# B vectors and tables of the state-space tiles made by POOL during the feed-forward, and doubled by ACT tile by tile

## The chip, the cores and the metric

The kernel runs on one core of one Trainium2 chip. Its engines are TensorE (PE), VectorE (DVE), ScalarE (ACT), GpSimd (POOL) and SyncE (SP), which here only issues transfers. The metric is the device time of one execution in microseconds, the median of several runs. The profile is of one execution more, taken by the hardware profiler.

## What is computed

One sequence of 256 tokens with 1,024 features goes through two layers of a first block (feed-forward, mixer, feed-forward) and two layers of a second block (attention, a dense feed-forward, a mixture of experts). The change touches only the mixer of the first block, and there only its S5 branch, a diagonal complex state-space model with 64 groups of 16 channels and 64 states:

```python
for i in range(DEPTH):                       # DEPTH = 2
    f = swiglu(rmsnorm(h, ffn1_pre_g[i]), ...)
    h = h + 0.5 * rmsnorm(f, ffn1_post_g[i])
    m = mixer(rmsnorm(h, mix_pre_g[i]), ...)  # ssd_branch and s5_branch
    h = h + rmsnorm(m, mix_post_g[i])
    ...
def s5_branch(u, ...):
    lam_bar = jnp.exp(lam * step)
    b_bar = ((lam_bar - 1.0) / lam)[..., None] * lax.complex(b_re, b_im)
    bu = jnp.einsum("blgc,gnc->blgn", ug, b_bar)
    _, states = lax.associative_scan(combine, (a_elems, bu), axis=1)
    y = jnp.real(jnp.einsum("blgn,gcn->blgc", states, c))
    ...
```

## The kernel before

All products are made from a high and a low part of each operand. For a chunk of weights (2,048 elements in each of 128 partitions) SP loads `raw`, ACT copies it to `w_hi` (line 1177), DVE subtracts to get `w_lo` (line 1634), and PE takes the chunk in three passes (lines 618 to 620, 671). Three slots go round, so the converts of a tick make the chunk that PE uses three ticks later. Each engine runs a program of its own, written out by hand in program order; only semaphores tie them together.

The first feed-forward has 11 steps (0 to 10) of three chunks. In a step, ACT applies SiLU twice, DVE makes `k_hi`, `stage` and `k_lo` of two hidden tiles (lines 1699 and 1687) and then converts. Behind some steps each engine does parts of the S5 set-up, by the tables handed to `ffn(...)`: DVE makes the powers and projections behind steps 6 and 7, the B vectors of tile 0 and a rotation table behind step 8, two more tables behind step 9. Then comes the post-norm and the next pre-norm: DVE lines 1675, 1677 (products with the gain, source in PSUM), 1680 (H updated), 1657 (H scaled into G), 1666 (low parts), with ACT between them; PE fills the time with `warm` matmuls (line 614), turns the stream (line 680) and starts the mixer.

The mixer goes in ticks, one chunk each: 4 for `u`, 1 for `dt`, 8 gates, 12 for the convolution, 8 for `z`. The S5 branch is spread over the ticks in 8 tiles of four pairs of groups. For tile t, PE turns the masked C (line 736) and the B vectors (line 743, `in_psum`) in tick 2t + 1, makes the local products (line 753, `local_psum`) and the chunk inputs (line 762) in tick 2t + 2, and the output (lines 774, 779) in tick 2t + 4. DVE makes the C vectors in tick 2t + 1 (`s5_cvecs`, lines 1859 to 1863) and scans in tick 2t + 3 (`s5_scan`, lines 1880 to 1894); tables for rotating the state (`s5_table`, lines 1872 to 1874) come in the ticks that `S5_TABLE_AT` names. In tick 7 DVE also makes the softplus of `dt` (`softplus_and_sums`), and taps of the convolution (line 1907) from tick 14 on. ACT masks the inputs (line 1291) and the diagonal (line 1300), fills the damping (line 1310), applies GELU (line 1315), evicts each chunk and converts. In tick 6 it waits twice for DVE (`dt_step`, lines 1370 and 1372).

POOL makes the B vectors of tiles 1 to 7 inside the mixer: two products of 512 elements once PE has turned the tile before (lines 2381, 2382), and once the local products of the tile before are through, a sum that writes each value twice, 1,024 elements (line 2385). Later it masks decays of the other branch (line 2372).

## Time and profile before

| what | us |
|---|---|
| median of three runs | 3162.09 |
| lowest and highest of them | 3159.95, 3169.51 |
| the profiled execution | 3172.73 |
| its span, first to last instruction | 3170.9 |
| PE busy | 3008.0 |
| DVE busy | 2228.4 |
| ACT busy | 1702.4 |
| POOL busy | 157.9 |

The granted clock of PE was 0.973 on average. In the page's 40 slices POOL works in four around 238 to 555 us and in three around 1110 to 1427 us: the two mixers of the first block, the only places with S5 tiles. Layer 1 repeats layer 0 about 897 us later. A row of a timeline gives start, duration, engine, line, operation, tiles and in brackets the idle time before it with what ended it.

### The profile page before, as it was taken

Reading aid. Unit: us, or ns where it says so; the run is one execution under the profiler, and the core shown is the slowest. Engines: PE = TensorE matmul, PEld = TensorE weight load, DVE = VectorE, ACT = ScalarE, POOL = GpSimd, SP = SyncE. Lnnn points to the kernel's source line nnn. Section 1 sums busy time; section 2 is a strip of 40 time slices with the busy share of each in tenths; the row PEclk is TensorE's granted clock in tenths of the full one; section 3 lists DMA queues with packets and bytes.
Section 4 is the critical chain, followed back from the end, with each engine's and each line's share of the span. In section 5 each row is a group of like instructions: output and inputs, shape, how many; then the busy total and the mean of one; then the engine's idle time right before and its main releaser. Section 6 shows DMA issues by size and latency. Waiting matters only on the chain.

```text
span 3170.9 us, 52654 instructions
## 1 busy us (share of the span) xinstructions
PE 3008.0 (95%) x20975; PEld 2688.3 (85%) x20975; DVE 2228.4 (70%) x2557; ACT 1702.4 (54%) x1966; POOL 157.9 (5%) x110
## 2 busy tenths in 40 slices
PE   8998999999989989998999999999799999999997
PEld 7998998989989978988989897999587877777776
DVE  5779975655557789957555555555568888888887
ACT  4445666334444456663344444444456776667665
POOL 0002213000000022030000000000000000000000
PEclk9998999999999999999999999999889999999999
DMA  7553352446545533533555453555079999999995
GB/s 227 173 156 92 111 155 81 157 139 208 174 154 194 167 112 94 143 111 107 168 170 194 163 186 120 186 171 181 6 260 363 330 342 350 327 326 344 351 326 200
DMA packets 488737, 619.92 MB, mean 196 GB/s; under 512 B 34689, under 2 KB 439059, under 8 KB 488595
## 3 DMA queue, kind: packets, MB, share of 16 engines
q1 hardware_dynamic: 488595, 617.91, 59.4%
q8 instruction: 104, 1.70, 0.2%
q14 instruction: 38, 0.31, 0.0%
HBM read 616.81 MB, written 1.05 MB: 195 GB/s over the span
## 4 chain that ended last, share of the span: by engine, by line
PE 76%; DVE 15%; ACT 4%; issue 3%; SPq 1%; DMA 0%; DVEq 0%; ACTq 0%
PE PS L1077 13%; PE PS L618 12%; PE PS L620 12%; PE PS L619 12%; PE PS L671 11%; DVE w_lo L1634 3%; PE PS L1102 3%; PE PS L1104 3%; PE PS L1103 3%; ACT w_hi L1177 1%; PE PS L1054 1%; ACT w_hi L1566 1%; PE PS L1112 1%; PE PS L800 1%; DVE act_out L1887 1%
## 5 line engine op out<-in xcount | busy, mean ns | idle before, releaser
L618 PE MATMUL PS<-x_hi,w_hi 128*128 128x256 f32 x3360 | 970.7, 289 | 17.7 <-DVE x_lo L1666 9.2
L619 PE MATMUL PS<-x_hi,w_lo 128*128 128x256 f32 x3360 | 961.4, 286 | 0.0
L620 PE MATMUL PS<-x_lo,w_hi 128*128 128x256 f32 x3360 | 960.8, 286 | 0.0
L1634 DVE TENSOR_TENSOR w_lo<-raw,w_hi 128x2048 fp32r<-128x2048 f32 x313 | 720.0, 2316 | 314.0 <-ACT w_hi L1177 313.3
L1177 ACT ACTIVATE w_hi<-raw 128x2048 fp32r<-128x2048 f32 x313 | 598.7, 1913 | 402.3 <-PE PS L671 249.0
L618 PEld LDWEIGHTS PS<-x_hi,w_hi 128*128 128x128 f32 x3360 | 656.3, 195 | 28.6 <-issue 13.3
L619 PEld LDWEIGHTS PS<-x_hi,w_lo 128*128 128x128 f32 x3360 | 656.5, 195 | 1.9
L620 PEld LDWEIGHTS PS<-x_lo,w_hi 128*128 128x128 f32 x3360 | 655.7, 195 | 0.0
L1077 PE MATMUL PS<-w_hi,x_hi 128*128 128x512 f32 x704 | 284.8, 405 | 3.1 <-DVE stage L2283 2.3
L1077 PE MATMUL PS<-w_lo,x_hi 128*128 128x512 f32 x704 | 276.4, 393 | 0.0
L1077 PE MATMUL PS<-w_hi,x_lo 128*128 128x512 f32 x704 | 274.9, 390 | 0.0
L1699 DVE TENSOR_TENSOR k_hi<-act_out,PS 128x256 fp32r<-128x256 f32 x110 | 46.2, 420 | 280.6 <-PE PS L620 279.0
L2277 DVE TENSOR_TENSOR w_lo<-raw,w_hi 128x2048 fp32r<-128x2048 f32 x96 | 219.9, 2290 | 32.6 <-ACT w_hi L1566 31.6
L2277 DVE TENSOR_TENSOR w_lo<-XC,w_hi 128x2048 fp32r<-128x2048 f32 x88 | 201.7, 2293 | 34.0 <-ACT w_hi L1566 31.8
L1566 ACT ACTIVATE w_hi<-raw 128x2048 fp32r<-128x2048 f32 x96 | 183.7, 1914 | 15.5 <-PE PS L1104 14.1
L671 PE MATMUL PS<-w_hi,k_hi 128*128 128x512 f32 x568 | 180.2, 399 | 6.4 <-DVE k_lo L1982 5.0
L671 PE MATMUL PS<-w_lo,k_hi 128*128 128x512 f32 x568 | 178.0, 395 | 0.0
L671 PE MATMUL PS<-w_hi,k_lo 128*128 128x512 f32 x568 | 177.3, 394 | 0.0
L1231 ACT ACTIVATE act_out<-PS 128x256 f32<-128x256 f32 x55 | 21.1, 384 | 279.2 <-PE PS L620 279.2
L1566 ACT ACTIVATE w_hi<-XC 128x2048 fp32r<-128x2048 f32 x88 | 168.2, 1912 | 1.2 <-DMA XC<-in_w_gu_moe_dram 1.2
L1077 PEld LDWEIGHTS PS<-w_hi,x_hi 128*128 128x128 f32 x704 | 132.6, 188 | 31.2 <-issue 3.7
L1077 PEld LDWEIGHTS PS<-w_lo,x_hi 128*128 128x128 f32 x704 | 132.4, 188 | 29.6
(410 smaller groups left out, 4715.0 us busy)
## 6 DMA issues: line engine op xcount, KB each, us to landing
XC<-in_w_gu_moe_dram SPq DMA_DIRECT2D x176, 512.0 KB, 8.9
raw<-in_w_gu_moe_dram SPq DMA_DIRECT2D x132, 512.0 KB, 7.9
raw<-in_w_in_dram SPq DMA_DIRECT2D x64, 1024.0 KB, 5.7
raw<-in_ffn_w_gate_dram SPq DMA_DIRECT2D x44, 1024.0 KB, 5.4
raw<-in_ffn_w_up_dram SPq DMA_DIRECT2D x44, 1024.0 KB, 6.4
raw<-in_ffn_w_down_dram SPq DMA_DIRECT2D x44, 1024.0 KB, 4.9
raw<-in_w_down_moe_dram SPq DMA_DIRECT2D x32, 1024.0 KB, 9.9
G<-in_w_down_moe_dram SPq DMA_DIRECT2D x32, 1024.0 KB, 9.5
```

The costliest lines, as they stand in the source:

```text
L618: mm(dst, w_hi[:, slot, w0:w0 + P], hi, start=start, stop=False, skip_group_check=True)
L619: mm(dst, w_lo[:, slot, w0:w0 + P], hi, start=False, stop=False, skip_group_check=True)
L620: return mm(dst, w_hi[:, slot, w0:w0 + P], lo, start=False, stop=True, skip_group_check=True)
L671: last = mm(PS[:, bank + 2 * t + b, :], left, right[:, slot, kt * D + 512 * b:kt * D + 512 * (b + 1)], start=False, stop=True, skip_group_ ...
L1077: last = mm(PS[:, 4, :], left, right, start=(k0 + k == 0 and right is whi and left is hi), stop=True, skip_group_check=True)
L1102: mm(PS[:, b, :], hi, whi, start=False, stop=True, skip_group_check=True)
L1103: mm(PS[:, b, :], lo, whi, start=False, stop=True, skip_group_check=True)
L1104: last = mm(PS[:, b, :], hi, wlo, start=False, stop=True, skip_group_check=True)
L1177: fn(w_hi[:, slot, :], raw[:, slot, :], ACT.Copy).then_inc(s["hi_ready"], n.one("hi_ready"))
L1566: fn(w_hi[:, MOE_SLOT[kind], :], MOE_RAW[kind][j % 3], ACT.Copy).then_inc(s["hi_ready"], n.one("hi_ready"))
L1634: tt(w_lo[:, slot, :], raw[:, slot, :], w_hi[:, slot, :].bitcast(F32), SUB)\
L2277: tt(w_lo[:, slot, :], MOE_RAW[kind][j % 3], w_hi[:, slot, :].bitcast(F32), SUB)\
```

## The change

POOL's program begins in the feed-forward. Once DVE has made the powers and projections (a new semaphore, `powers_ready`, behind step 7) and ACT the sines and cosines, POOL makes the five tables 0 to 4 and then the B vectors of tiles 0 to 4 in short form: 512 elements a tile, with the sum written once. DVE's `s5_first_bvecs` and the tables behind steps 8 and 9 and in ticks 0 and 1 are gone. ACT gets `s5_expand(t)`: it waits for `b_made` and copies the 512 elements of a tile to the 1,024 of `bvecs`, tile 0 behind step 9 of the feed-forward, tile t in tick 2t + 1. DVE waits for all five at the start of the mixer. Tiles 5 and 6 POOL makes after the fourth scan, tile 7 after the sixth doubling. The scratch of the norms' squares moves from `G` to `work`, since `G` now holds short B vectors. The core of the diff:

```diff
-S5_TABLE_AT = {0: 3, 1: 4, 4: 7, 6: 5, 8: 6}
+S5_TABLE_AT = {4: 7, 6: 5, 8: 6}
+S5_AHEAD = 5
...
-        weighted, scaled, unused = by_token(U5[:, :, :]), by_token(G[:, 0:8, :]), by_token(G[:, 8:16, :])
+        weighted, scaled = by_token(U5[:, :, :]), by_token(G[:, 0:8, :])
+        unused = wk(2368, 2, D)
...
+            def s5_expand(t):
+                act.wait_ge(s["b_made"], n.due("b_made"))
+                both = lambda x: x.rearrange("p (m c) -> p m c", c=16)[:, :, None, :].to_broadcast([P, 32, 2, 16])
+                fn(bvecs.rearrange("p w (q g c) -> p (w q) g c", q=4, g=2), both(b_homes[t]), ACT.Copy)\
+                    .then_inc(s["b_ready"], n.one("b_ready"))
...
-                else:
-                    act.wait_ge(s["b_ready"], n.due("b_ready"))
...
-                if i == 2:
-                    act.wait_ge(s["b_ready"], n.due("b_ready", S5_TILES - 1))
...
-                    for first, part in ((2, s5_inputs), (3, s5_diagonal), (0, s5_masked), (5, gelu)):
+                    for first, part in ((2, s5_inputs), (3, s5_diagonal), (1, s5_expand), (0, s5_masked), (5, gelu)):
...
-                ffn({3: (s5_exps,), 4: (s5_angles,), 6: (s5_tables,)})
+                ffn({3: (s5_exps,), 4: (s5_angles,), 6: (s5_tables,), 9: (lambda: s5_expand(0),)})
...
-                then(v.memset(damping[:, :, 0:1], 0.0))
...
+                v.memset(damping[:, :, 0:1], 0.0).then_inc(s["powers_ready"], n.one("powers_ready"))
+                dve.wait_ge(s["powers_ready"], n.last("powers_ready"))
...
+                dve.wait_ge(s["b_made"], n.due("b_made", S5_AHEAD))
...
-                     7: (s5_projections,), 8: (s5_first_bvecs, *tables_at(0)), 9: (*tables_at(1, 2), lambda: v.memset(local, 0.0))})
+                     7: (s5_projections,), 9: (lambda: v.memset(local, 0.0),)})
...
-                tt(a_, part(0), coef(powers_a), MULT)
-                then(tt(b_, part(1), coef(powers_b), MULT))
-                pair = lambda x: x.rearrange("p w q c -> p (w q) c")[:, :, None, :].to_broadcast([P, 32, 2, 16])
-                pool.wait_ge(s["local_psum"], n.due("local_psum"))
-                tt(bvecs.rearrange("p w (q g c) -> p (w q) g c", q=4, g=2), pair(a_), pair(b_), ADD)\
-                    .then_inc(s["b_ready"], n.one("b_ready"))
-                pool.wait_ge(s["b_ready"], n.last("b_ready"))
+                tt(dst, part(0), coef(powers_a), MULT)
+                then(tt(tmp, part(1), coef(powers_b), MULT))
+                tt(dst, dst, tmp, ADD).then_inc(s["b_made"], n.one("b_made"))
+                pool.wait_ge(s["b_made"], n.last("b_made"))
...
+                pool.wait_ge(s["powers_ready"], n.due("powers_ready"))
+                pool.wait_ge(s["table_ready"], n.due("table_ready"))
+                for t in range(5):
+                    s5_table(t)
+                for t in range(S5_AHEAD):
                     s5_bvecs(t)
...
+                pool.wait_ge(s["h5_ready"], n.due("h5_ready", 4))
+                s5_bvecs(5)
+                s5_bvecs(6)
+                pool.wait_ge(s["b_ready"], n.due("b_ready", 6))
+                s5_bvecs(7)
```

`s5_table` is the function that DVE had, word for word, with a scratch buffer of `work` as its temporary.

POOL's program in layer 0 before, from its first product for tile 1 in tick 2 of the mixer on:

```order
L2381 TENSOR_TENSOR G<-XC,work 128x512 [waits in_psum]
L2382 TENSOR_TENSOR G<-XC,work 128x512
L2385 TENSOR_TENSOR work<-G 128x1024 [waits local_psum,pool_step]
L2381 TENSOR_TENSOR G<-XC,work 128x512 [waits in_psum,b_ready]
L2382 TENSOR_TENSOR G<-XC,work 128x512
L2385 TENSOR_TENSOR work<-G 128x1024 [waits local_psum,pool_step]
```

And now, from the last of its five tables (lines 2373 to 2375), behind which come the B vectors of tiles 0 and 1:

```order
L2373 TENSOR_TENSOR XC<-work 128x512 [waits pool_step]
L2374 TENSOR_TENSOR work<-work 128x512
L2375 TENSOR_TENSOR XC<-XC,work 128x512 [waits pool_step]
L2383 TENSOR_TENSOR work<-XC,work 128x512 [waits pool_step]
L2384 TENSOR_TENSOR work<-XC,work 128x512
L2385 TENSOR_TENSOR work<-work 128x512 [waits pool_step]
L2383 TENSOR_TENSOR G<-XC,work 128x512 [waits b_made]
L2384 TENSOR_TENSOR work<-XC,work 128x512
L2385 TENSOR_TENSOR G<-G,work 128x512 [waits pool_step]
```

The waits for PE inside the mixer are gone, the operations are all of 512 elements, and nothing but POOL itself holds one back once the first has started.

DVE's program behind the converts of step 8 of the feed-forward, before: the B vectors of tile 0 and the first of three tables (the other two stood behind step 9).

```order
L1846 TENSOR_TENSOR work<-XC,work 128x512
L1847 TENSOR_TENSOR work<-XC,work 128x512
L1849 TENSOR_TENSOR work<-work 128x1024 [waits dve_step]
L1872 TENSOR_TENSOR XC<-work 128x512 [waits table_ready,b_ready]
L1873 TENSOR_TENSOR work<-work 128x512
L1874 TENSOR_TENSOR XC<-XC,work 128x512 [waits dve_step]
```

And now, behind step 9 up to the post-norm:

```order
L2066 MEMSET XC 128x512
L1705 TENSOR_TENSOR k_hi<-act_out,PS 128x256 [waits up_a,silu_done]
L1705 TENSOR_TENSOR stage<-act_out,PS 128x256
L1693 TENSOR_TENSOR k_lo<-stage,k_hi 128x256 [waits dve_step]
L1705 TENSOR_TENSOR k_hi<-act_out,PS 128x256 [waits chunk_used,silu_done]
L1705 TENSOR_TENSOR stage<-act_out,PS 128x256
L1693 TENSOR_TENSOR k_lo<-stage,k_hi 128x256 [waits dve_step]
L1640 TENSOR_TENSOR w_lo<-raw,w_hi 128x2048 [waits hi_ready] x2
L1681 TENSOR_TENSOR U<-PS,conv_out 128x1024 [waits chunk_used,gain_in]
```

The B vectors and the tables have left; the order of the rest is the same.

ACT's program in ticks 2 and 3 of the mixer, before (line 1300 masks the diagonal, line 1385 is the eviction, line 1177 the convert):

```order
L1385 ACTIVATE U<-PS 128x512 [waits chunk_used]
L1177 ACTIVATE w_hi<-raw 128x2048 [waits chunk_used,raw_c]
L1310 ACTIVATE rstd<-s5c 128x4x63 [waits b_ready]
L1300 ACTIVATE XC<-PS,con 32x4x16 [waits local_psum]
L1300 ACTIVATE XC<-PS,con 32x4x16 x7
L1385 ACTIVATE U<-PS 128x512 [waits chunk_used]
L1177 ACTIVATE w_hi<-raw 128x2048 [waits chunk_used,raw_a]
```

And now (lines 1304, 1391 and 1181 are the same operations, line 1312 is the doubling):

```order
L1391 ACTIVATE U<-PS 128x512 [waits chunk_used]
L1181 ACTIVATE w_hi<-raw 128x2048 [waits chunk_used,raw_c]
L1318 ACTIVATE rstd<-s5c 128x4x63
L1304 ACTIVATE XC<-PS,con 32x4x16 [waits local_psum]
L1304 ACTIVATE XC<-PS,con 32x4x16 x7
L1312 ACTIVATE work<-G 128x1024 [waits b_made]
L1391 ACTIVATE U<-PS 128x512 [waits chunk_used]
L1181 ACTIVATE w_hi<-raw 128x2048 [waits chunk_used,raw_a]
```

The doubling is new between the diagonal and the eviction, and line 1318 has lost its wait for `b_ready`.

## Rows read from the trace of the kernel before

**Rows 1.** Who waited for whom, PE, 230 to 400 us: total, times, longest.

```profile
PE PS L753 <- DVE work L1863: 8.2, 5, 2.4
PE PS L762 <- ACT XC L1291: 5.6, 1, 5.6
```

**Rows 2.** Windows, scan 0 to C vectors 7, both layers: length, busy PE, PEld, DVE, ACT, POOL, PE clock.

```profile
248.28:390.93 142.65, 124.82 (x1678) 120.33 (x1676) 134.66 (x160) 85.86 (x140) 35.88 (x18) 0.90 0.33 99
1145.27:1291.00 145.73, 124.08 (x1678) 119.50 (x1677) 138.92 (x160) 85.71 (x140) 37.85 (x18) 0.92 0.34 96
```

**Rows 3.** Timelines of DVE and POOL: start, duration, engine, line, operation, shapes, idle before.

```profile
229.11 0.69 DVE L1872 TENSOR_TENSOR XC<-work 128x512 f32<-128x512 f32 x1
...
236.84 1.49 DVE L1859 TENSOR_TENSOR work<-PS,work 128x1280 f32<-128x1280 f32 x1
236.98 1.11 POOL L2381 TENSOR_TENSOR G<-XC,work 128x512 f32<-128x512 f32 x1 [236.53 <-PE PS L743]
...
261.40 3.68 POOL L2385 TENSOR_TENSOR work<-G 128x1024 f32<-128x1024 f32 x1 [6.33 <-PE PS L753]
262.76 2.86 DVE L1872 TENSOR_TENSOR XC<-work 128x512 f32<-128x512 f32 x1
```

**Rows 4.** Timeline of DVE: softplus up to the scan; scan, taps, C vectors, next convert.

```profile
294.65 0.27 DVE L1917 TENSOR_SCALAR rows<-rows 32x256 f32<-32x256 f32 x1
...
300.65 0.67 DVE L1880 TENSOR_TENSOR work<-PS,XC 128x512 f32<-128x512 f32 x1
...
377.71 0.68 DVE L1880 TENSOR_TENSOR work<-PS,XC 128x512 f32<-128x512 f32 x1
...
383.51 2.71 DVE L1907 SCALAR_TENSOR_TENSOR conv_out<-conv_in,prm,conv_out 128x256 f32<-128x256 f32 x6
386.14 1.48 DVE L1859 TENSOR_TENSOR work<-PS,work 128x1280 f32<-128x1280 f32 x1
...
390.97 2.29 DVE L1634 TENSOR_TENSOR w_lo<-raw,w_hi 128x2048 fp32r<-128x2048 f32 x1
```

**Rows 5.** Timeline of DVE, its only idle times in the stretches of rows 2.

```profile
292.44 2.29 DVE L1634 TENSOR_TENSOR w_lo<-raw,w_hi 128x2048 fp32r<-128x2048 f32 x1 [4.06 <-ACT w_hi L1177]
...
354.77 2.29 DVE L1634 TENSOR_TENSOR w_lo<-raw,w_hi 128x2048 fp32r<-128x2048 f32 x1 [1.18 <-ACT w_hi L1177]
...
1189.48 2.29 DVE L1634 TENSOR_TENSOR w_lo<-raw,w_hi 128x2048 fp32r<-128x2048 f32 x1 [4.05 <-ACT w_hi L1177]
```

**Rows 6.** Groups by line with shapes apart, POOL: busy, mean ns, idle before.

```profile
L2385 POOL TENSOR_TENSOR work<-G 128x1024 f32<-128x1024 f32 x8 | 27.7, 3468 | 52.8 <-PE PS L753 52.8
```

**Rows 7.** Timelines of DVE and ACT, end of the feed-forward and the norms.

```profile
168.50 0.06 DVE L1839 MEMSET rstd<- 128x4 f32 x1
...
204.25 0.38 ACT L1231 ACTIVATE act_out<-PS 128x256 f32<-128x256 f32 x1 [5.38 <-PE PS L620]
...
208.33 4.49 DVE L1634 TENSOR_TENSOR w_lo<-raw,w_hi 128x2048 fp32r<-128x2048 f32 x2
...
215.66 2.48 DVE L1680 SCALAR_TENSOR_TENSOR H<-U,sums,H 128x1024 f32<-128x1024 f32 x2
216.98 1.06 ACT L1193 ACTIVATE G<-H 128x1024 f32<-128x1024 f32 x1 [1.55 <-DVE H L1680]
219.88 1.42 DVE L1657 TENSOR_SCALAR G<-H,sums 128x1024 f32<-128x1024 f32 x2
```

**Rows 8.** Timeline of PE: transposes and first chunks, before the mixer and before layer 1.

```profile
220.69 1.97 PE L680 MATMUL PS<-con,G 128*128 128x128 f32 x16 [1.23 <-DVE G L1657]
223.84 0.39 PE L618 MATMUL PS<-x_hi,w_hi 128*128 128x256 f32 x1 [1.18 <-DVE x_lo L1666]
...
235.64 0.38 PE L736 MATMUL PS<-con,stage 128*128 128x128 f32 x2
...
911.88 3.68 PE L680 MATMUL PS<-con,G 128*128 128x128 f32 x16 [7.72 <-DVE G L1657]
...
920.83 0.41 PE L618 MATMUL PS<-x_hi,w_hi 128*128 128x256 f32 x1
```

More of the change, by code:

```diff
@@ L1372, in mixer @@
                         fn(dt_rows[:, 3, :], dt_rows[:, 2, :], ACT.Ln).then_inc(s["dt_act"], n.one("dt_act"))
-                    for first, part in ((2, s5_inputs), (3, s5_diagonal), (0, s5_masked), (5, gelu)):
+                    for first, part in ((2, s5_inputs), (3, s5_diagonal), (1, s5_expand), (0, s5_masked), (5, gelu)):
                         t = s5_at(k, first)
-                        if t is not None:
+                        if t is not None and not (part == s5_expand and t == 0):
                             part(t)
@@ L1838, in s5_projections @@
                 v.memset(h5[:, :, :, 0:1], 0.0)
-                then(v.memset(damping[:, :, 0:1], 0.0))
-            def s5_first_bvecs():
-                q = slice(0, 4)
-                a_, b_ = (x[:, 0:512].rearrange("p (w q c) -> p w q c", w=8, q=4) for x in s5_tmp)
-                part = lambda r: b_raw[:, r, None, q, :].to_broadcast([P, 8, 4, 16])
-                coef = lambda x: x[:, q, :].rearrange("p q w -> p w q")[:, :, :, None].to_broadcast([P, 8, 4, 16])
-                tt(a_, part(0), coef(powers_a), MULT)
-                then(tt(b_, part(1), coef(powers_b), MULT))
-                pair = lambda x: x.rearrange("p w q c -> p (w q) c")[:, :, None, :].to_broadcast([P, 32, 2, 16])
-                tt(bvecs.rearrange("p w (q g c) -> p (w q) g c", q=4, g=2), pair(a_), pair(b_), ADD)                    .then_inc(s["b_ready"], n.one("b_ready"))
-                dve.wait_ge(s["b_ready"], n.last("b_ready"))
+                v.memset(damping[:, :, 0:1], 0.0).then_inc(s["powers_ready"], n.one("powers_ready"))
+                dve.wait_ge(s["powers_ready"], n.last("powers_ready"))
             def s5_cvecs(t):
@@ L2018, in mixer @@
                     convert((MIX + k) % RING)
-                n.given["b_ready"] += S5_TILES - 1
+                n.due("b_made", S5_TILES - S5_AHEAD)
                 ssd_inputs(7)
@@ L2069, in _ @@
                 pos[0] = -1
-                tables_at = lambda *tiles: tuple((lambda t=t: s5_table(t)) for t in tiles)
                 ffn({2: (s5_rows_a,), 3: (s5_rows_b,), 4: (s5_rows_c,), 5: (s5_columns, s5_turns), 6: (s5_powers,),
-                     7: (s5_projections,), 8: (s5_first_bvecs, *tables_at(0)), 9: (*tables_at(1, 2), lambda: v.memset(local, 0.0))})
+                     7: (s5_projections,), 9: (lambda: v.memset(local, 0.0),)})
                 post_norm()
@@ L2372, in ssd_masks, with s5_table @@
                     tt(d, d, gmask[:, (i // 2) % 2, :], MULT).then_inc(s["masked"], n.one("masked"))
+            def s5_table(t):
+                q = slice(4 * t, 4 * t + 4)
+                tmp = b_scratch[0].rearrange("p (q h l) -> p q h l", q=4, l=8)
+                dst = tables[t].rearrange("p q r (h l) -> p q (r h) l", l=8)
+                tt(dst, high_a[:, q, :, None].to_broadcast([P, 4, 16, 8]), low_cos[:, q, None, :].to_broadcast([P, 4, 16, 8]), MULT)
+                then(tt(tmp, high_b[:, q, :, None].to_broadcast([P, 4, 16, 8]), low_sin[:, q, None, :].to_broadcast([P, 4, 16, 8]), MULT))
+                then(tt(dst, dst, tmp, ADD))
@@ L2374, in s5_bvecs @@
             def s5_bvecs(t):
-                pool.wait_ge(s["in_psum"], n.due("in_psum"))
                 q = slice(4 * t, 4 * t + 4)
-                a_, b_ = (b_parts[t > 4][:, 512 * i:512 * (i + 1)].rearrange("p (w q c) -> p w q c", w=8, q=4) for i in range(2))
+                dst, tmp = (x.rearrange("p (w q c) -> p w q c", w=8, q=4) for x in (b_homes[t], b_scratch[t]))
                 part = lambda r: b_raw[:, r, None, q, :].to_broadcast([P, 8, 4, 16])
                 coef = lambda x: x[:, q, :].rearrange("p q w -> p w q")[:, :, :, None].to_broadcast([P, 8, 4, 16])
-                tt(a_, part(0), coef(powers_a), MULT)
@@ L2382, in s5_bvecs @@
-                then(tt(b_, part(1), coef(powers_b), MULT))
-                pair = lambda x: x.rearrange("p w q c -> p (w q) c")[:, :, None, :].to_broadcast([P, 32, 2, 16])
-                pool.wait_ge(s["local_psum"], n.due("local_psum"))
-                tt(bvecs.rearrange("p w (q g c) -> p (w q) g c", q=4, g=2), pair(a_), pair(b_), ADD)\
-                    .then_inc(s["b_ready"], n.one("b_ready"))
-                pool.wait_ge(s["b_ready"], n.last("b_ready"))
-            for l in range(DEPTH):
-                n.given["b_ready"] += 1
-                for t in range(1, S5_TILES):
-                    s5_bvecs(t)
-                n.due("in_psum")
-                n.due("local_psum")
+                tt(dst, part(0), coef(powers_a), MULT)
```

10 lines of the change are left out of this document (6 added, 4 removed).

## The prediction

> **What bounds the kernel now.** I read the list of waits of TensorE (PE) over layer 0's mixer first, then the windows that give each engine's busy time over the state-space part, then the timelines of DVE and POOL side by side. PE is busy nearly everywhere, so only its idle stretches matter. In the mixer it waits 8.2 us in five pieces for DVE's projected C vectors (line 1863) and 5.6 us in one for ACT's masked inputs, which hang on DVE too [rows 1]. From the first scan to the last C vectors, 142.65 us in layer 0 and 145.73 us in layer 1, DVE is busy 134.66 and 138.92 us, PE only 124.8 and 124.1 [rows 2]. DVE is the bound there.
>
> But DVE is not busy with work of its own all that time. A table operation takes 0.69 us alone and 2.86 us when it starts under POOL's 3.68 us operation; POOL's own span has grown as well, since it began under DVE's convert [rows 3]. A DVE operation with two SBUF sources and a POOL operation stand in turn, a whole instruction at a time. An operation that reads PSUM runs beside POOL at its usual 1.49 us [rows 3].
>
> **DVE's own work in the stretch.** A scan is 383.51 - 377.71 = 5.80 us, the taps 386.14 - 383.51 = 2.63, a tile's C vectors 390.97 - 386.14 = 4.83, the softplus 300.65 - 294.65 = 6.0 [rows 4]; a convert is 2.2 (two in 4.49 [rows 7]), a table three times 0.69, 2.07 [rows 3]. By the ticks there lie in it 12 converts (26.4), 7 scans (40.6), 7 sets of C vectors (33.8), the 3 tables of ticks 4, 6, 8 (6.2), two taps (5.3), the softplus (6.0) and two small operations (0.6, estimated at half a table operation each): 118.9 us. DVE waits for ACT's high parts 4.06 + 1.18 us in layer 0 and 4.05 in layer 1 [rows 5]. The rest, 142.65 - 118.9 - 5.2 = 18.5 us and 145.73 - 118.9 - 4.1 = 22.7 us, is what POOL costs DVE: 0.52 and 0.60 of POOL's busy 35.88 and 37.85 us [rows 2].
>
> **Part 1, the mixer.** POOL's B vectors of tiles 1 to 4 leave the mixer, and the doubling operation over 1,024 elements (mean 3.47 us [rows 6]) leaves POOL altogether. Tiles 5, 6 and 7 stay, in short form: 9 operations of 1.11 us [rows 3], 10.0 us of POOL. At the shares above (0.55) they cost DVE 5.5 us; the bounds are 2 us (all under operations that read PSUM) and 10 us (each in full). DVE's stretch becomes 118.9 + 5.5 + 4.1 = 128.5 us. The wait of 4.1 stays: ACT sits in tick 6 behind DVE's `dt_step` and then has its chain before the next high part, whatever POOL does. So layer 0 gains 142.65 - 128.5 = 14.2 us and layer 1 gains 17.2: 31.4 us. This counts on PE, which needs 124 us there with its slow pieces in, less than 128.5.
>
> ACT takes on the doubling: one copy of 1,024 elements a tile, 1.06 us by the row of the same length [rows 7]. It stands in the odd ticks behind the masking of the diagonal, which waits for PE in any case; behind it are queued the eviction and ACT's convert. PE wants the vectors after the whole chunk of that tick, some 5.9 us later (two chunks in 235.64 - 223.84 = 11.8 [rows 8]). I price it at nothing; if that cover went it would be 1.06 us x 7 a layer. The two tables leaving DVE's ticks 0 and 1 bring nothing: in both ticks DVE then waits for ACT or PE.
>
> **Part 2, the end of the feed-forward.** POOL starts when DVE has the powers, at 168.5 us [rows 7], and has 30 operations: 15 for five tables, 15 for five tiles. Up to the last convert's end, 212.8 us, there are 44.3 us. DVE has 8 converts and 6 small two-SBUF operations in that time (8 x 2.2 + 6 x 0.35 = 19.7 us, the small ones estimated at half a table operation), so POOL has 24.6 us for itself: at 1.11 us, and one semaphore step of about 0.1 (estimated) in three, 21 to 22 operations. Eight or nine are left when the post-norm begins. Within steps 8 and 9 the delays, one POOL operation before each convert, fall into DVE's waits; I charge 0.2 us a layer. In step 10 there is no such room: the two converts run straight into the post-norm, which PE waits for. One POOL operation goes before each: 2.2 us. The two updates of H (2.48 us [rows 7]) and the two scalings to G (1.42) come next on the path: half of four operations of 1.11, 2.2 us; the small low part 0.2. The sum is 4.6 us a layer. The bounds are 3.4 (the updates and scalings meet nothing more than one operation) and 9 (each of the seven meets one and POOL's operations are longer).
>
> The POOL work taken off DVE in steps 8 and 9 gives nothing, for DVE waits for PE there. ACT's first doubling stands between step 9's last convert and step 10's first SiLU and waits for the 18th POOL operation. At 1.11 us and under the converts that operation ends at about 203 us; the doubling then ends about 204, and ACT's second SiLU of that step starts at 204.25 in any case [rows 7]. Nothing, with little to spare (rival B). The wait of DVE at the mixer's start, for five tiles, is met: POOL is done at about 224 us, DVE gets there at 231 or later.
>
> **Part 3, the clock.** PE covers the post-norm with 32 dummy matmuls and idles 1.23 us before the turning of the stream at 220.69 [rows 8]. With 4.6 us more this idle is 5.8 us. In front of layer 1, after an idle of 7.72 us, the same 16 transposes took 3.68 us in place of 1.97, at the lower of the two clock levels (1.2 instead of 2.4 GHz), and the matmuls behind them started late as well: from the transposes' start to the 22nd matmul 920.83 - 911.88 = 8.95 us [rows 8]. At full clock it is 223.84 - 220.69 = 3.15 and 21 x 0.123 = 2.6, together 5.7. I charge 3.2 us a layer; the bounds are 0 (the clock holds over 5.8 us) and 4.
>
> **Sum.** -31.4 + 2 x (4.6 + 0.2 + 3.2) = -15.4 us. The profiled execution took 3172.7 us with a span of 3170.9, 10 us above the median of the three runs, and nothing in the sum depends on that; against the median 3162.1 - 15.4 = 3147 us.
>
> **What the Trainium skill would say.** POOL does the 512 elements in 1.11 us and DVE in 0.69, a ratio of 1.6 [rows 3]. The page "GPSIMD Engine Reference", section "3.1 Elementwise — side-by-side cycle accounting", gives 1.96 for a two-input operation over 2,048 elements. By that ratio each would be 1.35 us, an estimate of that page's, and the time would be that of rival A. The row is nearer, and the sum goes by it.
>
> **Rivals.**
> A, the lock only changes its place. Each moved operation that still meets DVE costs what it cost before, now at the norm where nothing covers it. If POOL's operations are 1.2 to 1.3 us long, 12 are left at 212.8 and each of the seven DVE operations meets one; a convert of steps 8 and 9 is late by 0.5 us or so. A layer pays 9 + 1 + 4 = 14, the sum is -31.4 + 28 = -3.4: 3159 us. For it speaks that DVE has no slack between 208.33 and 215; against it that POOL's short operation is 1.11. The Trainium skill ("Perfetto Trace Analysis", "Optimizing Scalar/DVE Operations") warns that work moved between these two engines may bring nothing, since they share a port; that is this rival.
> B, slower. ACT is held at its first doubling. It has room until about 204.5 us, by that SiLU; from there each us is PE's, because step 10's last products need the SiLU. With L us of lateness the change costs 2 x (L + 8) and breaks even at L = 7.7, which is POOL operations of about 1.5 us with these broadcast operands, which the trace shows only in another arrangement. At 1.7 us the 18th ends near 217, L = 12, and the norm loses 9: -31.4 + 2 x (12 + 9 + 1 + 4) = +20.6: 3183 us.
> C, the clock holds over the longer idle, or POOL's nine operations in the mixer hide under PSUM reads: -6.4 and -7: 3134 to 3141 us.
> D, something else bounds the mixer once DVE is lighter: PE after its slow pieces, or ACT with the doublings. Then the stretch is 132 us, the gain 24.5, the time 3154.
>
> **Chances.** Forecast (3141 to 3152) 0.46, C 0.16, A 0.16, D 0.12, B 0.10. The range reaches from C's lower end to above A: 3132 to 3164. A measurement of this kernel tells about 0.3%, 9.5 us, from no change. Faster by more: the forecast and C, 0.62. Within: A and D, 0.27 (with the weakest part of B). Slower: 0.11.
>
> **What would show it.** In the profile after: the stretch from scan 0 to C vectors 7 at about 128 us, with POOL's operations gone from ticks 3 to 8 and DVE's 2.86 us table at 0.69; the wait of PE for L1291's successor still there. POOL's 30 operations from 168.5 to about 224 us at 1.1 to 1.5 us each. The norm's DVE operations about 4.6 us later, PE's idle before the transposes 5 to 6 us and the granted clock at half behind it. Wrong it would be if ACT stood more than 6 us before its first doubling, if PE idled in step 10, or if the stretch stayed over 135 us.

## The result and the profile after

The changed kernel takes 3130.2 us (median of four runs, 3121.7 to 3136.2) where the kernel before takes 3162.6 (3160.0 to 3169.5). The ratio is 0.9891, with a 95% interval of 0.9875 to 0.9907. It is faster by 32.4 us, where 15.4 were forecast; the range ended at 3132, 1.8 us too high. The profiled execution took 3136.2 us with a span of 3134.4, so the two profiled executions lie 36.5 us apart.

The windows from scan 0 to the last C vectors answer to [rows 2], with the same columns:

```profile
249.10:378.81 129.71, 120.01 (x1626) 116.29 (x1625) 120.73 (x160) 89.89 (x145) 16.14 (x9) 0.95 0.35 109
1137.64:1265.00 127.36, 118.48 (x1686) 115.19 (x1684) 120.55 (x160) 91.40 (x146) 16.11 (x9) 0.96 0.38 111
```

142.65 us have become 129.71, and 145.73 have become 127.36: 12.9 and 18.4 us less, 31.3 together, where 31.4 were forecast. DVE's busy time fell by 13.9 and 18.4 us with the same 160 operations, so it was indeed waiting time inside busy operations that went. PE's clock rose from 0.90 and 0.92 to 0.95 and 0.96.

The timelines of POOL and DVE at the end of the feed-forward and in the norm, layer 0, answer to [rows 7] (start, duration, engine, line, operation, shapes, idle before):

```profile
165.83 1.07 POOL L2373 TENSOR_TENSOR XC<-work 128x512 f32<-128x512 f32 x1 [165.38 <-DVE rstd L1845]
...
173.29 3.00 POOL L2373 TENSOR_TENSOR XC<-work 128x512 f32<-128x512 f32 x1
176.26 3.11 POOL L2374 TENSOR_TENSOR work<-work 128x512 f32<-128x512 f32 x1
179.45 3.23 POOL L2375 TENSOR_TENSOR XC<-XC,work 128x512 f32<-128x512 f32 x1
...
185.00 1.31 POOL L2375 TENSOR_TENSOR XC<-XC,work 128x512 f32<-128x512 f32 x1
...
217.82 2.12 POOL L2385 TENSOR_TENSOR G<-G,work 128x512 f32<-128x512 f32 x1
```

```profile
171.98 9.54 DVE L1640 TENSOR_TENSOR w_lo<-raw,w_hi 128x2048 fp32r<-128x2048 f32 x3
...
205.71 6.52 DVE L1640 TENSOR_TENSOR w_lo<-raw,w_hi 128x2048 fp32r<-128x2048 f32 x2
212.15 1.21 DVE L1681 TENSOR_TENSOR U<-PS,conv_out 128x1024 f32<-128x1024 f32 x1
...
215.07 3.75 DVE L1686 SCALAR_TENSOR_TENSOR H<-U,sums,H 128x1024 f32<-128x1024 f32 x2
220.57 1.42 DVE L1663 TENSOR_SCALAR G<-H,sums 128x1024 f32<-128x1024 f32 x2
```

The turns can be read off. Alone, a product of a table lasts 1.07 us on POOL and its sum 1.31; under a convert each shows 3.0 to 3.2; three converts with POOL beside them take 9.54 us. In step 10 two converts take 6.52 instead of 4.49 us and the two updates of H 3.75 instead of 2.48. The product that reads PSUM (line 1681) is as short as ever, and so are the scalings into G, for POOL ended at 217.82 + 2.12 = 219.94 us.

PE and ACT around it answer to [rows 8] and [rows 7]: the transposes and first chunks of both layers, and ACT's first doubling.

```profile
221.38 3.68 PE L684 MATMUL PS<-con,G 128*128 128x128 f32 x16 [4.62 <-DVE G L1663]
225.61 0.43 PE L622 MATMUL PS<-x_hi,w_hi 128*128 128x256 f32 x1 [0.56 <-DVE x_lo L1672]
...
1112.60 0.58 PE L622 MATMUL PS<-x_hi,w_hi 128*128 128x256 f32 x1 [0.56 <-DVE x_lo L1672]
```

```profile
199.49 1.06 ACT L1312 ACTIVATE work<-work 128x1024 f32<-128x1024 f32 x1 [4.67 <-POOL work L2385]
200.46 0.36 ACT L1233 ACTIVATE act_out<-PS 128x256 f32<-128x256 f32 x1
```

PE idles 4.62 us before the transposes, which then run at the lower clock (3.68 us in place of 1.97). In layer 0 the clock is back for the first matmuls behind them (0.12 us apart); in layer 1 the first of them takes 0.58 us. PE's list of waits from 230 to 390 us answers to [rows 1]:

```profile
PE PS L747 <- DVE work L1875: 3.5, 1, 3.5
PE PS L766 <- ACT XC L1295: 3.5, 1, 3.5
PE PS L757 <- DVE work L1859: 2.7, 3, 1.8
```

The wait for the C vectors (now line 1859) is down from 8.2 us to 2.7.

The next table cuts every profiled execution at the same operations of DVE. "Norm" runs from the powers (POOL's start) over step 10 and the norms to scan 0, "stretch" from scan 0 to the start of the last C vectors (4.8 us shorter than the windows above). Both are given for layer 0 and layer 1, and "rest" is all else.

| kernel | norm | stretch | rest | span |
|---|---|---|---|---|
| before | 79.8, 79.8 | 137.9, 141.0 | 2732.5 | 3170.9 |
| before_again | 79.8, 79.8 | 140.3, 141.0 | 2723.9 | 3164.8 |
| changed | 83.4, 84.9 | 124.9, 122.6 | 2718.6 | 3134.4 |
| after_again | 83.1, 84.7 | 122.9, 122.6 | 2717.5 | 3130.9 |
| bvecs_only | 79.7, 79.7 | 122.6, 122.6 | 2713.5 | 3118.1 |
| short_in_mixer | 78.8, 78.8 | 129.3, 129.4 | 2713.8 | 3130.2 |
| no_pool_in_mixer | 85.0, 84.9 | 121.4, 120.6 | 2708.7 | 3120.5 |
| nine_more_behind | 83.6, 85.1 | 123.0, 122.6 | 2720.7 | 3135.0 |
| nine_more_ahead | 93.9, 91.6 | 122.9, 122.6 | 2708.8 | 3139.8 |
| warm48 | 91.3, 91.3 | 123.0, 122.6 | 2716.2 | 3144.3 |
| warm24 | 82.3, 82.3 | 124.9, 122.6 | 2710.3 | 3122.5 |
| step_early | 79.7, 79.6 | 118.8, 118.8 | 2714.2 | 3111.1 |
| before_no_pool | 78.8, 78.8 | 120.7, 120.7 | 2711.9 | 3110.9 |
| softplus_behind | 79.7, 79.7 | 119.5, 119.2 | 2721.8 | 3119.9 |

The rest spreads over 13 us among the kernels other than before, which do the same there. From the last C vectors in layer 0 to the powers of layer 1 the traces show 678.7 us with 13.7 us lost to the lower clock, and 670.5 us with 5.1 lost, for one and the same kernel (changed, after_again). I take such losses as the length times one minus the granted clock, summed over short windows. The length without them is 665 us both times. So the norm and the stretch are what a single trace can tell; the rest it can't.

### The profile page after: what moved, and what is told of

Same layout as the page of the kernel before. It is cut to its first block, busy times and chain, and to the rows that moved or that the text cites. A ratio compares the mean times of both kernels' runs of the same rounds, so it can differ in the third digit from the quotient of the medians.

```text
span 3134.4 us, 52666 instructions
## 1 busy us (share of the span) xinstructions
PE 2988.7 (95%) x20975; PEld 2672.7 (85%) x20975; DVE 2189.0 (70%) x2521; ACT 1716.8 (55%) x1982; POOL 211.7 (7%) x146
## 4 chain that ended last, share of the span: by engine, by line
PE 78%; DVE 14%; ACT 4%; issue 3%; DVEq 0%; DMA 0%; SPq 0%; ACTq 0%
PE PS L1081 13%; PE PS L622 12%; PE PS L623 12%; PE PS L624 12%; PE PS L675 11%; DVE w_lo L1640 3%; PE PS L1106 3%; PE PS L1108 3%; PE PS L1107 3%; ACT w_hi L1181 1%; PE PS L1058 1%; ACT w_hi L1572 1%; PE PS L804 1%; PE PS L1116 1%; DVE act_out L1881 1%
## 5 line engine op out<-in xcount | busy, mean ns | idle before, releaser
L1640 DVE TENSOR_TENSOR w_lo<-raw,w_hi 128x2048 fp32r<-128x2048 f32 x313 | 730.0, 2349 | 303.1 <-ACT w_hi L1181 302.4
L2271 DVE TENSOR_TENSOR w_lo<-raw,w_hi 128x2048 fp32r<-128x2048 f32 x96 | 219.8, 2289 | 32.6 <-ACT w_hi L1572 32.4
```

What stands on the lines that cost most here:

```text
L1640: tt(w_lo[:, slot, :], raw[:, slot, :], w_hi[:, slot, :].bitcast(F32), SUB)\
L2271: tt(w_lo[:, slot, :], MOE_RAW[kind][j % 3], w_hi[:, slot, :].bitcast(F32), SUB)\
```

## Experiments

### The two kernels once more

> The changed kernel once more, word for word. Expected: 0.989 of before again, 3125 to 3135 us. The stretch from scan 0 to the last C vectors again 129.7 and 127.4 us within 1 us, the way from POOL's start to the post-norm again 2.2 us longer than before in both layers. If the 2.8 us that the changed kernel was ahead before POOL had started (165.69 in place of 168.50) and the 5.6 us of layer 1's last third are chance, they differ here; if they belong to the change they repeat.

Measured: 3132.5 us (five runs), ratio 0.9896 (0.9877 to 0.9914).

> The kernel before once more, word for word, for its trace alone: which stretches repeat and which do not. Expected: scan 0 to the start of the last C vectors 137.9 and 141.0 us within 1, post-norm to the low parts 10.2, first low part to scan 0 25.4. If the long way from layer 0's last C vectors to layer 1's powers (679.35 us) and from layer 1's last C vectors to the end (1884.6) come out otherwise, the 10 us between the profiled execution and the median are in them.

Measured: a span of 3164.8 us. In both kernels the norm repeats within 0.3 us and layer 1's stretch within 0.1; layer 0's differs by 2.0 us between the traces of the changed kernel and by 2.5 between those of before. The 2.8 us by which the changed kernel was ahead at the powers are chance: all traces together reach that point between 164.3 and 168.5 us, before_again at 167.1. The 5.6 us of layer 1 did not repeat either: from the last C vectors of layer 1 to the end the second trace of the changed kernel took 1880.7 us, the first 1874.2.

### Only the B vectors on POOL

```diff
-S5_TABLE_AT = {4: 7, 6: 5, 8: 6}
+S5_TABLE_AT = {0: 3, 1: 4, 4: 7, 6: 5, 8: 6}
...
-                     7: (s5_projections,), 9: (lambda: v.memset(local, 0.0),)})
+                     7: (s5_projections,), 8: tables_at(0), 9: (*tables_at(1, 2), lambda: v.memset(local, 0.0),)})
...
-                pool.wait_ge(s["table_ready"], n.due("table_ready"))
-                for t in range(5):
-                    s5_table(t)
```

> POOL makes only the B vectors of tiles 0 to 4 in the feed-forward (15 operations in place of 30), DVE makes the tables where it made them before. Theory (the cost of the change is POOL's work that reaches into step 10 and the norm): POOL is done by about 192 us, the two converts of step 10 take 4.5 us again, PE idles 1.2 us before the transposes at full clock, the stretch from scan 0 to the last C vectors stays at 128 to 130 us. Gain over the changed kernel 3.5 + 1.1 us in layer 0 and 3.4 + 2.6 in layer 1: 10.6 us, to about 3120 us. Rival (DVE has no room for tables 3 and 4 in ticks 0 and 1 any more): the first scan comes 2 to 4 us later a layer than the norm's end allows, and the gain is 3 to 6 us.

Measured: 3123.8 us (five runs), ratio 0.9868 (0.9846 to 0.9890); the changed kernel, measured beside it, 3132.5. Windows of layer 0 from the powers to the post-norm, and from there to the low parts (columns as in [rows 2]), first the changed kernel's:

```profile
165.69:212.15 46.46, 46.46 (x315) 43.26 (x314) 33.74 (x31) 20.47 (x18) 45.06 (x26) 1.00 0.49 160
212.15:224.68 12.53, 7.91 (x38) 6.99 (x36) 7.84 (x9) 4.87 (x11) 7.56 (x5) 0.77 0.31 98
```

```profile
165.69:210.76 45.07, 44.68 (x305) 41.45 (x304) 39.19 (x39) 19.49 (x17) 26.79 (x15) 1.00 0.49 160
210.76:220.94 10.18, 8.70 (x48) 7.31 (x46) 6.58 (x9) 5.86 (x13) 0.00 (x0) 1.00 0.45 139
```

With 15 operations POOL is out of the way before step 10, and the norm takes its old 10.18 us at full clock. From the powers to the post-norm it is 45.07 us, 0.8 more than in the kernel before: here DVE makes tables in steps 8 and 9 too, and POOL's turns there do show. The stretch is what it was in the changed kernel, 122.6 us. The norm column of the table falls by 3.7 and 5.2 us, 8.9 together (10.6 were expected), and the medians by 8.7. The rival, that DVE has no room for two tables in ticks 0 and 1, is out: from the low parts to scan 0 it takes 24.42 us, as without them. The tables on POOL bring nothing and cost all that the norm pays.

### Only the short form and the doubling

```diff
+        b_homes = [wk(3904, 512)] + [flat(G[:, 12:14, :])] * 4 + [
...
-                pool.wait_ge(s["table_ready"], n.due("table_ready"))
-                for t in range(5):
-                    s5_table(t)
-                for t in range(S5_AHEAD):
+                s5_bvecs(0)
+                for t in range(1, S5_TILES):
+                    pool.wait_ge(s["in_psum"], n.due("in_psum"))
+                    if t == 7:
+                        pool.wait_ge(s["b_ready"], n.due("b_ready", 6))
                     s5_bvecs(t)
...
```

The tables are on DVE here, as in bvecs_only.

> Half of the change: ACT doubles as in the changed kernel, but POOL makes the B vectors of tiles 1 to 7 in the mixer, in the ticks where it made them before, in short form; tables on DVE as before. Theory (POOL's busy time in the stretch times 0.55 is what DVE loses): 21 operations of 1.11 us, 23.3 us, cost 12.8; the stretch is 118.9 + 12.8 + 4.1 = 135.8 us, between before (142.65, 145.73) and the changed kernel (129.7, 127.4); the norm is as before. In time about 2 x 8.4 = 17 us under before, 3145. Rival (it was the 1,024-element operation that hurt, since it started under a convert and blocked the C vectors): the stretch is 131 us or less, the time 3130.

Measured: 3132.6 us (six runs), ratio 0.9898 (0.9875 to 0.9922). Windows of the stretch (to the start of the last C vectors), in this kernel, in the kernel before and in before_no_pool (below):

```profile
243.16:372.49 129.33, 117.61 (x1593) 114.42 (x1592) 119.77 (x155) 87.92 (x141) 24.74 (x18) 0.92 0.37 112
```

```profile
248.28:386.14 137.86, 121.71 (x1600) 117.50 (x1599) 129.97 (x155) 81.62 (x134) 35.88 (x18) 0.90 0.34 102
```

```profile
244.30:364.95 120.65, 113.74 (x1588) 110.90 (x1587) 111.51 (x155) 80.41 (x134) 0.00 (x0) 0.96 0.39 119
```

The stretch to the end of the C vectors is 134.1 us (129.3 + 4.8), where the theory said 135.8 and the rival 131 or less: nearer the theory. POOL still makes 18 operations there. But the time as a whole, which I had put at 3145 and the rival at 3130, is that of the changed kernel. Norm and stretch account for 23 of the 35 us gained, on the mean of the two traces of before; the remainder is of the kind left open below. Without POOL at step 10 the norm is short (78.8 us), so what the stretch loses against the changed kernel (6.1 us a layer) the norm gives back (5.2). In the change as it was made, then, B vectors and tables together, moving POOL's work out of the mixer has brought nothing measurable. What it gains net is what this kernel gains too: the third operation, 1,024 elements on POOL behind a wait for the local products, became 512 without that wait and a copy on ACT. Which of the two it is, the length or the wait, this run does not separate.

That does not hold for the B vectors alone. The kernel bvecs_only differs from this one in where POOL makes them. Its stretch is 6.7 us a layer shorter (122.6 for 129.3), its norm 0.9 longer, and its median is 8.8 us lower. So the move is worth something; in the changed kernel the tables, moved along, eat it up at the norm.

### What POOL costs in the mixer, before and after

The kernel before with POOL's `s5_bvecs` emptied:

```diff
-                tt(a_, part(0), coef(powers_a), MULT)
-                then(tt(b_, part(1), coef(powers_b), MULT))
...
-                tt(bvecs.rearrange("p w (q g c) -> p (w q) g c", q=4, g=2), pair(a_), pair(b_), ADD)\
-                    .then_inc(s["b_ready"], n.one("b_ready"))
-                pool.wait_ge(s["b_ready"], n.last("b_ready"))
+                pool.sem_inc(s["b_ready"], 1)
+                n.given["b_ready"] += 1
```

> The kernel before with POOL's operations in the mixer left out: the B vectors of tiles 1 to 7 are not computed, those of tile 0 stay in the buffer; POOL only waits and signals. Theory (POOL's 35.9 us a layer cost DVE 18.5 to 22.7 us of the stretch, and ACT's doubling costs nothing): from scan 0 to the start of the last C vectors 137.9 to 141.0 us fall to 120.6 to 121.4, as in the kernel without POOL's nine operations, where ACT doubles. If it comes out at 117 or less, the doubling on ACT does cost 4 us a layer or more; if at 125 or more, something else than POOL was in before's stretch.

Measured: 3111.0 us (four runs), ratio 0.9838 (0.9812 to 0.9864), stretch 120.65 and 120.68 us.

The changed kernel without the nine operations that POOL has left in the mixer:

```diff
-                s5_bvecs(5)
-                s5_bvecs(6)
+                pool.sem_inc(s["b_made"], 2)
+                n.given["b_made"] += 2
                 pool.wait_ge(s["b_ready"], n.due("b_ready", 6))
-                s5_bvecs(7)
+                pool.sem_inc(s["b_made"], 1)
+                n.given["b_made"] += 1
```

> The changed kernel with POOL's nine operations for tiles 5 to 7 left out: the B vectors of these tiles are not computed, ACT doubles what lies in their buffers. Theory: the stretch falls by the 5.5 us that they were priced at, to 123 to 124 us a layer, and the time by 11 us. Rival (PE, busy 124 us, bounds it then, or the nine lay under operations that read PSUM): it falls by 2 us or less a layer.

Measured: 3126.4 us (four runs), ratio 0.9876 (0.9855 to 0.9897), stretch 121.4 and 120.6.

Both end at the same stretch, one with ACT's doubling and one without: the doubling is hidden. POOL's work cost the kernel before 17.2 and 20.3 us of the stretch. DVE's busy time without it is 111.5 us, so before it held 18.5 and 22.8 us of waiting for POOL. The prediction had worked out 18.5 and 22.7, and that agreement is luck: it took DVE's own work 2.6 us too high and its idle time too low (5.2 and 4.1 us, where the stretch of before has 7.9 and 6.7). The nine operations that are left cost 2.2 us a layer (123.25, the mean of four stretches, less 121.0), not 5.5: about what the rival said. They add 4.4 us to DVE's busy time (115.9 for 111.5), but the stretch grows by half of that only; the other half comes off DVE's idle time.

### POOL at work through the norm, and ahead of the first doubling

```diff
                 for t in range(S5_AHEAD):
+                    if t == S5_AHEAD - 1:
+                        for again in range(3):
+                            s5_table(4)
                     s5_bvecs(t)
```

> The changed kernel with nine POOL operations more (table 4 three times again) ahead of the B vectors of tile 4, so that POOL works on through the norm. Theory of the forecast (the scaling of H into G meets POOL as well): the two scalings take 3.6 us in place of 1.42, post-norm to low parts 14.7 in place of 12.5 us, and with the clock 2 to 4 us a layer in all. Rival (an operation with one SBUF tensor and a scalar a row does not take turns with POOL): the scalings stay at 1.42 us, and the norm costs what it did.

Measured: 3131.8 us (four runs), ratio 0.9897 (0.9870 to 0.9923). The scalings into G:

```profile
219.06 2.55 DVE L1663 TENSOR_SCALAR G<-H,sums 128x1024 f32<-128x1024 f32 x2
```

They take 2.55 us in place of 1.42 (I had expected 3.6): an operation with a single SBUF tensor takes turns with POOL too, once for the two. The rival is out. This agrees with the Trainium skill: the page "SBUF — State Buffer", section "🔬 SBUF: two separate sides", has DVE and GpSimd share one pair of ports under an exclusive lock, taken by DVE operations with two SBUF inputs or in a two-port mode, for a whole instruction; the products from PSUM at 1.21 us fit it as well. But the norm lengthens by 0.3 us only (12.80 for 12.53 us from post-norm to low parts, where I had expected 14.7), since PE begins the transposes after the first scaling and at the low clock needs longer than the second takes. So even with POOL at work there, the scalings would have cost the norm 0.3 us, and not the 1.1 that is their half of my 2.2.

```diff
-                for t in range(5):
+                for t in (0, 1, 2, 3, 4, 4, 4, 4):
                     s5_table(t)
```

> The changed kernel with nine POOL operations more (table 4 three times again) ahead of all B vectors. Theory (rival B of the prediction, ACT held at its first doubling): tile 0 is ready 10 to 12 us later, at 210 us instead of 199.5, the first SiLU of step 10 stands behind it, PE idles 6 to 9 us in step 10, and the time grows by 15 to 24 us with the norm's part. If it grows by less than 8, ACT's place behind step 9 has more room than the prediction gave it.

Measured: 3144.6 us (eight runs), ratio 0.9947 (0.9931 to 0.9963). ACT's doubling and the matmul of step 10 behind it:

```profile
208.84 1.06 ACT L1312 ACTIVATE work<-work 128x1024 f32<-128x1024 f32 x1 [15.24 <-POOL work L2385]
```

```profile
211.46 1.22 PE L675 MATMUL PS<-w_hi,k_hi 128*128 128x512 f32 x2 [8.32 <-DVE k_lo L1693]
```

Rival B of the prediction is a real mechanism. The doubling starts 10.6 us later after the powers (208.84 - 164.47 = 44.4 for 199.49 - 165.69 = 33.8) and PE idles 8.32 us: the room was 2.2 us, where the prediction had about half a microsecond. Up to the post-norm the kernel takes 9.0 and 8.1 us longer than the changed one, in the median 13 us (against 3131.8 with the nine behind, measured beside it), a little under the 15 to 24 expected. Still it is faster than the kernel before, since the gain of the stretch stands against it.

### The clock

```diff
                 ffn(rows=True)
-                warm(4, 16)
+                warm(4, 48)
```

> The changed kernel with 48 dummy matmuls in place of 16 at the place ahead of the transposes of the norm. Theory (the idle of 4.6 us is what lets the clock fall): PE idles 1.2 us there, the transposes take 1.97 us, low parts 1.1 us earlier, the way from there to scan 0 is 24.4 us in both layers (25.97 and 24.42 in the changed kernel). Gain 2 to 5 us a kernel: 3128 us. Rival (the clock falls anyhow): nothing.

Measured: 3145.6 us (six runs), ratio 0.9946 (0.9928 to 0.9964). I had mis-sized it: 32 dummy matmuls more are not 3.4 us but 11.3, and the norm grew to 91.3 us. It tells only the price of one, 0.35 us, and that with PE busy the way to scan 0 is 24.40 us in both layers.

> The changed kernel with 24 dummy matmuls in place of 16 ahead of the transposes (the profile shows each as two: 48 for 32). With 48 in place of 16 the post-norm to the first low part grew from 12.5 to 20.4 us, so one costs 0.35 us on PE (11.3 us for 32, with the 4.6 us of idle used up first 3.4): eight are 2.8 us. Theory: PE idles 1.8 us before the transposes, they take 1.97 us, the first low part comes 11.4 to 11.5 us after the post-norm's start, and from there to scan 0 it is 24.4 us in both layers (24.4 to 26.0 in the changed kernel). Gain 2 to 5 us over the changed kernel. Rival (the clock falls anyhow): nothing.

Measured: 3127.0 us (five runs), ratio 0.9874 (0.9852 to 0.9896).

```profile
219.99 1.97 PE L684 MATMUL PS<-con,G 128*128 128x128 f32 x16 [1.17 <-DVE G L1663]
```

The idle is 1.17 us, the transposes take 1.97, and the norm column is 82.3 in both layers, 1.1 and 2.6 us less than in the changed kernel: the clock term. It is the idle that lets the clock fall, and a few more dummies take it back. How long it stays down is not the same each time: in layer 0 of two executions of the same kernel it was back by the end of the transposes, in layer 1 of both some 17 matmuls later, and in no_pool_in_mixer, which does the same there, late in both layers (norm 85.0 and 84.9).

### What bounds the mixer next

This kernel is bvecs_only with one operation of DVE in another place:

```diff
-                    if k == 6:
-                        dve.wait_ge(s["dt_act"], n.due("dt_act"))
-                        ts(dt_rows[:, 2, :], dt_rows[:, 1, :], 1.0, None, ADD).then_inc(s["dt_step"], n.one("dt_step"))
                     t = s5_at(k, 3)
                     if t is not None:
                         s5_scan(t)
+                    if k == 5:
+                        dve.wait_ge(s["dt_act"], n.due("dt_act"))
+                        ts(dt_rows[:, 2, :], dt_rows[:, 1, :], 1.0, None, ADD).then_inc(s["dt_step"], n.one("dt_step"))
```

> bvecs_only (POOL makes the B vectors of tiles 0 to 4 in the feed-forward, DVE all tables) with one DVE operation moved: the second dt_step, that ACT waits 5.9 us for in tick 6, stands in tick 5 between scan 1 and the C vectors of tile 2, and no longer at the head of tick 6. Theory (ACT's wait in tick 6 is what DVE's 4.1 us for the high part and PE's 3.5 and 2.7 us hang on): ACT waits under 1 us there, DVE's wait falls under 1 us, PE's two waits under 1.5 us together, the stretch from scan 0 to the start of the last C vectors falls from 122.6 to 117 to 119 us a layer. Time 3123.8 - 2 x 4.5, about 3115. Rival (PE is the bound by now): the waits move to another line and the time stays at 3120 or above.

Measured: 3112.0 us (five runs, 3111.0 to 3115.3), ratio 0.9828 (0.9808 to 0.9847), the fastest complete kernel of this study. ACT's second step in the changed kernel and here:

```profile
279.68 0.42 ACT L1378 ACTIVATE rows<-rows 32x256 f32<-32x256 f32 x1 [5.93 <-DVE rows L1990]
```

```profile
268.77 0.42 ACT L1378 ACTIVATE rows<-rows 32x256 f32<-32x256 f32 x1
```

The 5.93 us are gone, and with them PE's wait for the masked inputs; DVE's for the high part is down to 1.1 us. The stretch fell from 122.6 to 118.8 us a layer, as the theory said, and the rival is out. But PE kept a long wait between 245 and 380 us, beside 1.4 us in three short ones; the expectation was under 1.5 us in all:

```profile
PE PS L747 <- DVE work L1877: 5.1, 1, 5.1
```

It hangs on scan 2, which stands behind the softplus in tick 7. The last kernel turns these two round.

```diff
-                    if k == 7:
-                        softplus_and_sums()
                     t = s5_at(k, 3)
                     if t is not None:
                         s5_scan(t)
+                    if k == 7:
+                        softplus_and_sums()
```

> step_early with the softplus of tick 7 behind scan 2 in place of ahead of it. In step_early PE waits 5.1 us in tick 7 for that scan to have read its inputs. Theory (DVE's own work is the bound: 118.9 us and about 2 for POOL's nine, of the 123.6 from scan 0 to the end of the last C vectors): PE's wait falls under 1 us, but the stretch from scan 0 to the start of the last C vectors falls by 0 to 2.6 us only, 116.2 to 118.8, and the time by 5 us at most. Rival (PE's wait was the last one that counted): the stretch falls by 4 us or more, to 114 or less, the time to 3104 or less.

Measured: 3120.9 us (five runs), ratio 0.9847 (0.9823 to 0.9871). The stretch is 119.5 and 119.2 us, not shorter, and the list of waits from 245 to 380 us reads

```profile
PE PS L757 <- DVE work L1859: 6.5, 3, 5.5
```

PE's wait did not fall under 1 us as expected, it moved to the C vectors. DVE is busy 116 of 119.4 us, so it is the bound and PE's waits only show where. That fits the theory, though its range for the stretch (116.2 to 118.8) is missed by 0.4 and 0.7 us, and the rival is out. At a stretch 0.5 us longer than step_early's, the 9 us between the medians are not from here: two of the five runs took 3109.1 and 3109.4 us, less than any of step_early, and three 3120.9 to 3121.7. The trace is one of the three; it has 7.6 us more in the rest, 5 of them time lost to the lower clock. The order of the two operations is not shown to cost anything.

## Why the prediction was wrong

The direction and the mechanism were right, but the gain forecast, 15.4 us, was half of what was measured. The step that failed is the price of the norm: parts 2 and 3 charged 16.0 us for it, and it cost 8.7. The lower-clock time behind the stretch was put at nothing, and part of the miss stays open. By the steps of the prediction, on the two profiled executions:

**Part 1, the mixer: 31.4 us forecast, 31.3 measured.** The sum holds, but three of its terms were off and cancelled. To the start of the last C vectors, DVE's own work is 111.5 us where I had 118.9 - 4.8 = 114.1. POOL's nine operations cost 2.2, not 5.5: I carried the share of 0.55 over from a POOL program of long operations, and the bound "all under PSUM reads", 2 us, was the better value. And DVE's idle time without POOL is 9.1 us (120.65 - 111.5), not 4.1: three waits for ACT's high parts make 7.1 of it, and the rest is short gaps between operations. That the sum came out within 0.1 us is luck.

**Part 2, step 10 and the norm: 4.8 us a layer forecast, 3.5 measured.** The converts were right (2.2 forecast, 2.0 measured). The updates of H took 1.27 us more, and the scalings nothing, since POOL was done at 219.94 and not at 224. That is the term mis-sized: eight or nine operations were to be left at the post-norm, and 26 of 30 had been issued when it began. I had counted the small operations of DVE as blocking POOL, which they hardly do, and the converts at 2.2 us each: eight converts at 1.95 us of waiting (3.0 to 3.2 for 1.1 to 1.3) are 15.6 of the 46.5 us, and the other 30.9 hold 26 operations at 1.19. My time for POOL was 24.6.

**Part 3, the clock: 3.2 us a layer forecast, 1.1 and 2.6 measured.** The low parts came 3.30 us after the transposes' start instead of 2.22, and from there to scan 0 layer 0 lost nothing and layer 1 1.5 us. The idle before it was 4.62, not 5.8. I had taken the row in front of layer 1, after 7.72 us of idle, as if the clock stayed down as long after a shorter one.

**Not counted, ahead of scan 0: 0.96 us a layer.** Three POOL operations of tile 1 stood there ([rows 3] has the first), and the third, over 1,024 elements, lengthened the convert ahead of the scan, in the kernel before:

```profile
245.11 3.25 DVE L1634 TENSOR_TENSOR w_lo<-raw,w_hi 128x2048 fp32r<-128x2048 f32 x1 [1.15 <-ACT w_hi L1177]
```

Without them it is 24.42 us from the low parts to scan 0, with them 25.37. In short_in_mixer three short ones stand there and it is 24.41, so it was the long one. I let the gain begin at scan 0.

With these the norm cost 3.6 and 5.1 us where 16.0 together were forecast: 7.3 us of the miss. The Trainium skill's ratio that stood against my durations ("GPSIMD Engine Reference", "3.1 Elementwise — side-by-side cycle accounting", 1.96) was not borne out for two of the three operations of 512 elements: 1.07 to 1.11 us on POOL to 0.69 on DVE is 1.6. For the sum it nearly was: 1.31 to 0.69 is 1.9. Rival A, which took 1.2 to 1.3 us for all, fell because only four operations, and not 12, were still to be issued at the post-norm; its time for one was off by little (1.19 with the gaps).

**Not counted, behind the stretch: 3.7 us.** From the last C vectors to the copy of `dt_tok` 67.36 us became 65.12 and 65.79 became 64.30. Before, PE waited there for the last C vectors and then ran 10.9 us at a granted clock of 0.78 (layer 0) and 10.7 us at 0.84 (layer 1):

```profile
386.14:397.00 10.86, 9.12 (x170) 8.52 (x169) 10.65 (x14) 9.45 (x17) 0.00 (x0) 0.78 0.23 62
1286.29:1297.00 10.71, 9.41 (x179) 8.81 (x178) 10.50 (x14) 9.31 (x17) 0.00 (x0) 0.84 0.23 61
```

```profile
374.02:385.00 10.98, 10.98 (x206) 10.59 (x205) 10.77 (x14) 9.05 (x19) 0.00 (x0) 1.00 0.24 70
```

So a shorter wait can be a gain in clock too, behind the wait itself. I priced the clock only where the change made it worse. But not all of the 3.7 us repeats: before_again took 64.29 and 65.78 us there, after_again 64.29 twice. Layer 1's 1.5 us came in both pairs of traces, layer 0's 2.2 only in the first.

**Open: some 5 to 11 us.** Norm, stretch and what follows make -31.4 + 8.7 - 3.7 = -26.4 of the 36.5 us between the profiled executions, and 32.4 between the medians. The other 10 of the profiled pair are chance as far as can be seen: 2.8 ahead of the powers, the rest in lower-clock time far from the change. But such a remainder is left of nearly every median. With norm, stretch and the way to the copy of `dt_tok`, all on the mean of the two traces of before, bvecs_only should gain 38 us and gains 44; warm24 29 and 39; step_early 46 and 54; before_no_pool 43 and 54; the changed kernel, on the mean of its two traces, 28 and 32 or, measured again, 35. The two traces of before lost 60 and 50 us to the lower clock outside norm and stretch, the twelve others 30 to 50. Whether shorter waits early on let the clock hold later, or two traces are too few, no run here tells.

## What to carry to other kernels

Between DVE and POOL, cost a move by what stays on POOL as much as by where it goes. Here the kernel in which only the 1,024-element operation was shortened and freed of its wait, its doubling given to ACT, ran as fast as the whole change. Moving the B vectors ahead was worth 6.7 us of the stretch a layer for 0.9 of the norm, and moving the tables with them took that back. Move only what has a hole to go into: 15 operations fitted, 30 ran into the norm, and 39 held up an engine that everything waits for. And where a wait of PE is taken away, look at the clock behind it too: in layer 1 here 1.5 us came from there, in both pairs of traces.

## What the runs showed of the hardware

A DVE operation and a POOL operation alternate, so a group of DVE operations in a row pays about one POOL operation each at most: three converts 9.54 us for 6.7, two updates 3.75 for 2.48, two scalings 2.55 for 1.42 (one for the pair), products from PSUM nothing. The time that the profile gives a POOL operation includes its wait: 3.0 to 3.2 us under a convert for 1.07 to 1.31 alone. After an idle of 4.6 us the clock's return differed from layer to layer and from run to run: by the end of the transposes, or some 17 matmuls later, 1.5 us apart. A stretch of unchanged program took 670.5 to 679.3 us in the 14 traces with 5 to 15 us lost to the lower clock, and 664 to 667 without these losses, so they make most of what one execution differs from the next there.
